# Six hand-overs between engines in a two-network float32 kernel

## The reference

```
for i in 0, 1:                                   # first network
    mix = latent attention + stick-breaking attention      (i = 0)
        = forgetting attention, 16 heads                   (i = 1)
    x = layer_norm(a * x + mix)
    x = layer_norm(a * x + (silu(x w1) * (x w3)) w2)       # width 2816
    x = x + sigmoid(x w_gate + b) * (p w_proj)
mod = silu(c) w_ada + b_ada                      # second network, conditioned by c
h   = modulate(rms_norm(x), mod)
mix = [retention(4 heads), sparse attention(8 heads)] w_out
      # sparse attention: compressed + selected + window branch, each gated
x   = x + ga1 * mix
h   = modulate(rms_norm(x), mod)
x   = x + ga2 * experts(h)    # 16384 single-row experts, 8 heads choose 16 each
return rms_norm(x)
```

## Time and profile before

| | us |
|---|---|
| median of 3 runs | 1767.23 |
| lowest and highest | 1764.0, 1768.93 |
| profiled execution, its own time | 1767.16 |
| its span | 1765.6 |
| PE busy | 1711.5 |
| DVE busy | 1314.8 |
| ACT busy | 968.7 |
| POOL busy | 230.2 |

### The profile page before, as it was taken

The page is one execution under the profiler, slowest core; times in us unless marked ns, Lnnn a source line. Parts: engine busy times, 40 slices in busy tenths (PEclk is TensorE's granted clock), DMA queues, the critical chain, the costliest instruction groups (busy, mean ns, idle before and its releaser), DMA issues.

```text
span 1765.6 us, 30099 instructions
## 1 busy us (share of the span) xinstructions
PE 1711.5 (97%) x10188; PEld 1508.3 (85%) x10188; DVE 1314.8 (74%) x2519; ACT 968.7 (55%) x1782; POOL 230.2 (13%) x158
## 2 busy tenths in 40 slices
PE   9899999999999998998989999999999999999998
PEld 8778888799888887897989999999998887888886
DVE  5468877777779777867667794888997666666666
ACT  5645554465555543556445546988885444333333
POOL 2010000013200000122115786000000000000001
PEclk9999999999999999999999999999999999999999
DMA  7524757655547676444234455444445555555554
GB/s 243 183 111 154 264 190 264 224 168 203 191 139 265 208 268 236 156 144 143 84 108 156 168 184 174 144 144 144 143 144 181 188 190 181 196 194 190 192 196 136
DMA packets 86354, 317.49 MB, mean 180 GB/s; under 512 B 9632, under 2 KB 9904, under 8 KB 85488
## 3 DMA queue, kind: packets, MB, share of 16 engines
q1 hardware_dynamic: 77328, 279.48, 47.0%
q10 hardware_dynamic: 7200, 25.45, 4.0%
q0 software_dynamic: 1728, 11.25, 1.8%
HBM read 315.08 MB, written 1.05 MB: 179 GB/s over the span
## 4 chain that ended last, share of the span: by engine, by line
PE 63%; DVE 7%; ACT 5%; issue 2%; DMA 1%; POOL 0%; ACTq 0%; DVEq 0%; POOLq 0%
PE bank L260 12%; PE bank L262 12%; PE bank L261 12%; PE bank L2163 9%; PE bank L2167 5%; PE bank L1147 5%; PE bank L2393 3%; DVE wl L199 2%; PE bank L1151 2%; ACT wh L192 2%; DMA ada<-in_w_ada 1%; PE bank L353 1%; DVE ss_s L595 1%; ACT ss_p L603 1%; ACT ss_p L601 0%
## 5 line engine op out<-in xcount | busy, mean ns | idle before, releaser
L192 ACT ACTIVATE wh<-ring 128x1024 fp32r<-128x1024 f32 x526 | 555.7, 1058 | 564.3 <-PE bank L262 362.2
L199 DVE TENSOR_TENSOR wl<-ring,wh 128x1024 fp32r<-128x1024 f32 x476 | 586.5, 1235 | 286.2 <-ACT wh L192 284.9
L260 PE MATMUL bank<-wh,xs 128*128 128x512 f32 (+1 forms) x796 | 286.3, 360 | 3.3 <-DVE wl L199 2.5
L262 PE MATMUL bank<-wh,xs 128*128 128x512 f32 (+1 forms) x796 | 282.1, 354 | 0.0
L261 PE MATMUL bank<-wl,xs 128*128 128x512 f32 (+1 forms) x796 | 282.1, 354 | 0.0
L2163 PE MATMUL bank<-xs,wh 128*128 128x512 f32 x736 | 250.8, 402 | 0.0
L1147 PE MATMUL bank<-xs,wh 128*128 128x512 f32 x704 | 223.0, 396 | 3.7 <-DVE xs L381 2.3
L260 PE MATMUL bank<-xs,wh 128*128 128x256 f32 x632 | 182.0, 288 | 1.8 <-DVE xs L381 0.9
L262 PE MATMUL bank<-xs,wl 128*128 128x256 f32 x632 | 178.8, 283 | 0.0
L261 PE MATMUL bank<-xs,wh 128*128 128x256 f32 x632 | 178.7, 283 | 0.0
L260 PEld LDWEIGHTS bank<-wh,xs 128*128 128x128 f32 x796 | 151.9, 191 | 27.5 <-DVE wl L199 5.0
(11 more groups left out here) (481 smaller groups left out, 2820.8 us busy)
## 6 DMA issues: line engine op xcount, KB each, us to landing
ring<-in_stream SPq DMA_DIRECT2D x529, 512.0 KB, 3.3
ada<-in_w_ada ACTq DMA_DIRECT2D x48, 512.0 KB, 4.7
rows<-in_rows POOLq DMA_DIRECT2D x1, 2560.0 KB, 11.4
rows<-in_rows POOLq DMA_DIRECT2D x2, 1024.0 KB, 5.0
con<-in_early POOLq DMA_DIRECT2D x1, 1374.0 KB, 14.4
x_feature_major<-in_x_fm SPq DMA_DIRECT2D x4, 256.0 KB, 6.7
x<-in_x_tm POOLq DMA_DIRECT2D x1, 1024.0 KB, 5.2
weighted<-in_subkeys POOLq DMA_DIRECT2D x1, 1024.0 KB, 5.3
```

The source lines that it names most:

```text
L192: C.activation(wh[q % AHEAD][:, :], ring[slot][:, :], ACT.Copy).then_inc(s_high, 1)
L199: low.tensor_tensor(wl[q % AHEAD][:, :], ring[slot][:, :], wh[q % AHEAD][:, :], ALU.subtract).then_inc(s_low, 1)
L260: T.matmul(o, left[0], right[0], start=start, stop=False, skip_group_check=True)
L262: return T.matmul(o, left[1], right[0], start=False, stop=stop, skip_group_check=True)
```

## The change

Six edits, none of which adds or removes arithmetic:

1. The barrier behind the logarithms of the first mixer waits for what was issued before them, and for ACT's logarithms no longer.
2. In both feed-forwards the two `residual_half` calls move from between the projections into the second one, behind its pieces 0 and 2.
3. The turning of the selected keys ks moves from between the two pieces of rq0 to between the two pieces of kw.
4. In step 1 of the last stream the rope of rq1 moves behind two compressed pieces and the low part of the window.
5. In step 4 `cmp_values` moves behind the last compressed piece of the keys and its row copy.
6. In `pair` the parts of the next up tile move ahead of the weighing of this down tile.

```diff
--- before.py
+++ after.py
@@ -291,13 +291,15 @@
     def no_need(k):
         pass
 
-    def project(left, nk, dst, width=HALF, need=no_need, hold=False, by_token=False):
+    def project(left, nk, dst, width=HALF, need=no_need, hold=False, by_token=False, behind=()):
 
 
         if width == HALF:
             for j in range(nk // 2):
                 done = two_k(dst, j, nk, left, need_x if left[0] is xh else need, hold and 2 * j + 2 == nk,
                              by_token and 2 * j + 2 == nk)
+                if j % 2 == 0 and j // 2 < len(behind):
+                    behind[j // 2]()
             return done
 
         def products(h, l):
@@ -896,10 +898,12 @@
         for t, b in ((0, 2), (1, 6)):
             sv_in = dve.did(V.tensor_copy(apart(sbv, slice(t, t + 1)),
                                           bank[b][:, :].rearrange("p (t h d) -> p t h d", t=1, h=NH)))
+        before_logs = issued()
         for h0 in range(0, NH, 2):
             act.wait(ex[h0 + 1])
             ln = act.did(C.activation(lz[:, h0:h0 + 2, :], lz[:, h0:h0 + 2, :], ACT.Ln, bias=1.0))
-        release()
+        for lane in (act, dve, pool):
+            lane.wait(*before_logs)
         scope.close()
 
         for lane in (pe, dve):
@@ -1256,9 +1260,8 @@
         gated_in = lambda k: pe.wait((s_gate, 5 * max(k + 1, KF - 2)))
         ada["of"] = (3, 4) if layer else (1, 2)
         y = project((hh, hl), KF, sums[0:2], need=gated_in)
-        for t in range(NT):
-            residual_half(z, st, 0, t, y, sums[t])
-        y = project((hh, hl), KF, sums[2:4], need=gated_in, hold=True, by_token=True)
+        behind = [lambda t=t, y=y: residual_half(z, st, 0, t, y, sums[t]) for t in range(NT)]
+        y = project((hh, hl), KF, sums[2:4], need=gated_in, hold=True, by_token=True, behind=behind)
         return first_token["done"], y, sums, (phh, pll, p_ready)
 
     GATES, PROJS = ([bank[3], bank[5]], [bank[6], bank[7]]), ([bank[0], bank[2]], [bank[1], bank[4]])
@@ -1680,7 +1683,9 @@
                                     .broadcast_to([P, 2, 2, DH]), ACT.Copy))
     vs_in = act.did(C.activation(nvs[:, :, :, DH:P], by_token(bank[3])[:, :, P:QC].rearrange("p t (g d) -> p t g d", g=2), ACT.Copy))
     turn_quarter("nq1", 1, bank[0], nqT[:, 2:4, :], read["nq1"])
-    y = both(bank[4])
+    quarter(bank[4], (xh, xl), 0, need_x)
+    turn_key_apart("ks", bank[0], added["ks"], turned_in["nq1"])
+    y = quarter(bank[4], (xh, xl), 4, need_x)
     pair_ab = rope_quarter("kw", bank[4], 2, DH, "n", y)
     doubled("kw", *pair_ab, 0)
     act.wait(read["kw"])
@@ -1694,7 +1699,6 @@
     turn_shifted("kc", bank[3], added["kc"], vs_in)
     pe.wait(ga1_done)
     quarter(bank[6], (xh, xl), 0, need_x, meantime=lambda y: windows_low("vc"))
-    turn_key_apart("ks", bank[0], added["ks"], turned_in["nq1"])
     y = quarter(bank[6], (xh, xl), 4, need_x)
     rotated_quarter("rq0", bank[6], 2, RDK, "r", y, 2)
     turn_key_apart("kw", bank[1], added["kw"], turned_in["nq0"])
@@ -1943,12 +1947,12 @@
             product["rq1"] = quarter(bank[7], (xh, xl), 4, need_x,
                                      meantime=lambda y: windows_sum("kc", "pe_k", added["win", "vc"]))
         elif st == 1:
-            rotated_quarter("rq1", bank[7], 2, RDK, "r", product["rq1"], 3)
             windows_high("kc")
             pe.wait(gd)
             cmp_piece("vc", 0, bank[5])
             cmp_piece("vc", 1, bank[5])
             windows_low("kc")
+            rotated_quarter("rq1", bank[7], 2, RDK, "r", product["rq1"], 3)
         elif st == 2:
             cmp_piece("vc", 2, bank[5])
             cmp_piece("vc", 3, bank[5])
@@ -1961,9 +1965,9 @@
             cmp_piece("kc", 1, bank[6])
         elif st == 4:
             cmp_piece("kc", 2, bank[6])
-            cmp_values(bank[5])
             cmp_piece("kc", 3, bank[6])
             cmp_row("kc", bank[6])
+            cmp_values(bank[5])
         elif st == 5:
             pe.wait(turned_in["rq1"])
             quarter(bank[7], (xh, xl), 0, need_x)
@@ -2547,10 +2551,9 @@
         q = q1 + 2 * u
         down_wide(q, s, u + LEAD, n)
         split(q + AHEAD, i)
-        weigh(q, s, u, n, first=i is None and u < 3)
-
         V.wait_ge(s_weighed, n + u)
         parts(u + 1, n, None if i is None and u < 2 else q - 2, s)
+        weigh(q, s, u, n, first=i is None and u < 3)
         if i is None and u == 0:
             T.wait_ge(s_wm, ROUTES)
         up(q + 1, s, u, n)
```

## The result

The changed kernel takes 1756.68 us (median of 6 runs, 1755.57 to 1761.0) against 1768.43 us for the kernel before in the same comparison (6 runs, 1764.0 to 1770.08). The ratio is 0.9949, 95% interval 0.9931 to 0.9966: some 9 us faster. The forecast was 1760.4 with a range of 1755 to 1766. The saving came out above the 6.8 us forecast in both comparisons, but 6.8 us lies within both intervals (6.0 to 12.2 us and 4.8 to 10.2).

A forecast was written before the change was run, and what follows sets the result against it. TensorE, busy 97% of the span, was taken as the bound. Terms 1.4 + 0.8 + 1.9 + 0 + 1.6 + 0.4 = 6.1 us plus 0.7 for the clock gave 1767.2 - 6.8 = 1760.4 us, range 1755.0 to 1766.0.

The forecast's parts named there:

- My term for the keys: Selected keys, last mixer: turning them sooner wins 1.9 us of a 2.40 us gap and 1.7 us lost clock; bounds 0.8 to 2.4.
- the 0.7 us: Whole kernel: net gain from falls of the clock beside the closed gaps, with one new long gap possibly bringing one.
- the 0.8 foretold: Behind the first mixer's barrier: TensorE's gap of 1.87 us falls to about 0.8 us.
- Rival (d): Barrier: the change does nothing there, as the softplus still waits for the logarithms; 1.4 us missing; 25% shared with another rival.
- The upper bound of 3.1: Barrier: most the edit could win, 3.1 us, with the fall of the clock gone; the term itself was 1.4 us.
- The slack of 0.6 us: Second feed-forward: the following low part, done at 671.1, comes 0.6 us before PE wants it, if the weights have landed.
- cost nothing there: Selected keys: four transposes and two copies move to where ACT and DVE wait for PE, at no cost.
- Both gaps as foretold: Rope, last stream: gaps of 2.05 and 2.27 us become about 1.4 and 2.8, same total, so 0 gain.
- by this rule alone: Rope: DVE operations with both inputs in SBUF and GpSimd SBUF reads exclude each other; new order would win 1.0 us; not taken.
- rival (a): Clock: falls go beyond the count, above all the one at 838 us; 3.4 us more, 1757.0 us; 15%.
- PE never waits: Expert loop: ACT waits 1.58 us for PE in each pair, PE never, so nothing is won inside the loop.
- Rival (c): Expert loop: weighing behind 0.7 us of parts delays each of 28 pairs, 19.6 us in all, 1780.0 us; 5%.

The follow-up runs named there:

- both comparisons: Unchanged changed kernel against the kernel before, timed twice: 1756.68 against 1768.43 us, ratio 0.9949; later 1759.90 against 1767.32 us, ratio 0.9957.
- the rope put back: Changed kernel with the rope of rq1 back at its old place: 1758.83 us, ratio to before 0.9954.
- the rope in the slot: Changed kernel with rq1's rope moved to where DVE waits for the third unit's exponentials, its transposes one step later: 1757.82 us, ratio to before 0.9956.
- the kernel before with the gap bridged: Kernel before with eight unused identity transposes added on TensorE in the 1.65 us gap before rk0's transposes: 1764.94 us, ratio 0.9991.
- all three mixer edits: Kernel before with only the keys, rope and values edits of the last mixer: 1762.52 against 1767.04 us, ratio 0.9989.
- the outer edits: Kernel before with only the barrier, residual sums and pair edits, none in the last mixer: 1762.08 us, ratio 0.9974.

## Why the prediction was right

The direction and the range were right, and so was, in the main, the mechanism of each edit but that on the keys. That the gaps summed up as forecast is partly luck: the keys came out 1.4 us too high, and feed-forward, rope and pairs together 1.1 to 1.9 us too low. My term for the keys also held the fall of the clock behind its gap, so the 0.7 us was not all that I had put down to the clock. Gap parts below are taken between profiles with equal low clock in the stretch; each rests on few profiles, and the edits of barrier, feed-forward and pairs were timed together only.

| place | forecast | gaps, measured | from |
|---|---|---|---|
| barrier | 1.4 | 1.4 | mean of five 109.80, of nine 108.37 |
| feed-forward | 0.8 | 1.3 to 1.9 | 17.72 to 18.32, now 16.40 |
| keys | 1.9 | 0.5 | 74.75 to 74.27 |
| rope | 0 | 0.2 to 0.4 | 34.59 to 34.15, see the rope put back |
| values | 1.6 | 1.7 | 34.88 to 34.38, 21.65 to 20.41 |
| pairs | 0.4 | 0.8 | 598.2 to 597.4 |
| sum | 6.1 | 5.9 to 6.7 | |
| clock, net | 0.7 | about 2 | below |

**Barrier.** Right as worked out, 0.77 us of gap for the 0.8 foretold. Rival (d) falls. The upper bound of 3.1 does not exist: the low clock behind the barrier costs nothing. In three of the five profiles with the old order it came already at 79 us, ahead of the 1.87 us gap, which was then gone. Three of the nine profiles with the change have 3.4 us of it there and take 108.37 to 108.40 us, the other six 108.34 to 108.37. TensorE's gaps over the stretch come to 8.5 us in these six and to 7.0 to 7.1 in the three: the slower matmuls take up time in which it would have waited.

**Feed-forward.** The term was too small for two reasons. I took the gap from one profile: in the five profiles with the old order it is 1.07, 1.42, 1.42, 1.65 and 1.83 us, as the conditioning weights land sooner or later; in the nine with the new order there is none, and the stretch is 16.40 us in each (the fifth of the old ones, 20.30 us, has a fall of the clock in it). And closing a gap wins some 0.25 us more than the gap's own length: 17.72 - 16.40 = 1.32 us for the gap of 1.07, 1.68 for that of 1.42 and 1.92 for that of 1.65, as the shown gap begins at the modelled end of a matmul, which in an unbroken run overlaps the next. The slack of 0.6 us that I worked out behind the second low part sufficed in all of them.

**Keys.** This step failed. I said that the four transposes "cost nothing there" at their new place, and that the clock's fall behind the gap goes. The transposes take 0.5 us of TensorE ahead of everything that ACT and DVE wait for there. The following low part and high part show it (before, with the next low part and the rope, then after):

```profile
775.76 1.23 DVE L199 TENSOR_TENSOR wl<-ring,wh 128x1024 fp32r<-128x1024 f32 x1 [2.61 <-ACT wh L192]
...
779.78 0.60 PE L1624 MATMUL bank<-keep,kdup_kw 128*128 128x128 f32 x4
779.82 1.06 ACT L192 ACTIVATE wh<-ring 128x1024 fp32r<-128x1024 f32 x1
...
780.91 1.23 DVE L199 TENSOR_TENSOR wl<-ring,wh 128x1024 fp32r<-128x1024 f32 x1 [1.51 <-ACT wh L192]
...
784.15 0.69 DVE L1571 TENSOR_TENSOR rope_n<-bank,con 128x512 f32<-128x512 f32 x1
```

```profile
771.83 1.22 DVE L199 TENSOR_TENSOR wl<-ring,wh 128x1024 fp32r<-128x1024 f32 x1 [2.61 <-ACT wh L192]
...
775.30 0.60 PE L1627 MATMUL bank<-keep,kdup_kw 128*128 128x128 f32 x4
...
775.88 2.01 ACT L192 ACTIVATE wh<-ring 128x1024 fp32r<-128x1024 f32 x2
...
776.97 2.36 DVE L199 TENSOR_TENSOR wl<-ring,wh 128x1024 fp32r<-128x1024 f32 x2 [1.51 <-ACT wh L192]
```

The two come 3.93 and 3.94 us earlier, when TensorE at the transposes of kw is 4.48 us earlier. Behind them DVE wins 0.96 us (from the low part at 780.91 to the rope 3.24 us before, from that at 776.97 to the rope at 779.25 2.28 after), and so the rope comes 4.90 us earlier, 0.4 more than TensorE's own shift, not 0.8. The new gap of 2.15 us was foretold to 0.05 us, and it is what keeps the edit at 0.5 us. The rest of my 1.9 was the fall of the clock, which can be there with either order: the first profile of before has it (75.80), the second has not (74.75), and the rope in the slot, which has the keys edit, has it again (75.66). So it costs 1.05 us with the old order and 1.4 with the new, and where it falls the edit wins 0.2 us at most, by this one profile.

**Rope.** Both gaps as foretold (1.4 and 2.8; 1.65 and 2.73), the whole 0.2 to 0.4 us better. The two low parts, apart from POOL's sum, take 2.36 us together and the sum 1.26, against 3.44 and 2.19 in the earlier trace rows, so the price of running together that the Trainium skill (SBUF — State Buffer, Who interferes with whom) leads one to expect is in the trace; by this rule alone the edit would have won 1.0. It won 0.2 to 0.4, as DVE then stood 0.56 us waiting for ACT's high part (791.75 above) before the low parts.

**Values.** The gap part was right, 1.7 for 1.6. Behind it stood more: where the clock falls after the 1.65 us gap, it costs 3.16 us (24.81 against 21.65). The fall stood in two of the four profiles with that gap and in none of the ten without it, one of which is the kernel before with the gap bridged. That suggests, and fourteen profiles can't show, that the gap makes the fall likelier without making it certain. Half of 3.16 is 1.6 us; the times agree with that (1.6 us won by bridging the gap, 2.2 us won by the values alone beyond their gaps), but their intervals also hold nothing for either. If it is so, my rival (a) was half right and should have entered the sum at half its price.

**Pairs.** I missed half. The step from "PE never waits" in the loop overlooked the loop's start: the first up product waited 0.17 us for its low part, and the parts ahead of the weighing win 0.4 us there (the gap and, as in the feed-forward, 0.25 us more) as they do at the end. Rival (c) falls: the 28 pairs lost nothing.

**Clock.** I priced each fall at 1.7 us for 3.4 us of low clock. It costs that only where TensorE is what everything waits for: 3.16 us for 6.8 at the compressed scores, about 1.8 for 3.4 in the one feed-forward that had it (20.30 us with a gap of 1.83), 1.05 to 1.4 for 3.4 in the first unit, 0.0 to 0.2 at 802 us in units 2 to 4 (34.88 with and without), nothing behind the barrier or at 880 to 890 us (the stretch from 850 to 900 us takes 49.5 us with 3.4 and 49.3 to 49.6 with 6.8). Over the runs, the low time worked out from each run's granted clock (twice one minus the clock, times the span) is 30 to 32 us in the mean before, and 25 and 27 us in the two sets of the changed kernel; the clock is given to 0.001, which is 3.5 us of low time in a single run. In the 33 runs of before that go with the first experiments the span rises by 0.36 us with each us of it (a straight line through them); 5 us less is 1.8 us, an estimate. With the gaps that makes 7.7 to 8.5 us, about what the two comparisons show. Which edit takes the low time away is not shown: it is 28.5 us with the values alone, where before had 32.2, but 30.3 with all three mixer edits, where before had 30.2, and 26.7 with the outer edits. What I drew from the Trainium skill (TensorE: Matmul & The Clock Gate, What's actually happening), whose statement is that the gate's bookkeeping does not start anew with the kernel, was that a fall at a given gap may be there in one execution and not in the next, and this agrees with these traces: 24.81 and 21.65 us for the same gap.

**What stays open.** The comparisons lie 0.8 and 2.2 us above the forecast saving, less than their intervals, so the times alone don't show that the clock was undersized. 1.5 us of the difference of the two profiles lies in stretches that the change doesn't touch. From 183.6 to 317.9 us one and the same instructions take 134.3 us in five profiles and up to 138.1 in the others, and around the layer norms at 336 and 698 us it is 49.3 to 51.3 and 34.3 to 38.0. Pieces of the stream and of the conditioning weights land there sooner or later, and whether the changed kernel does so less often can't be told from fourteen profiles.

## What to carry to other kernels

Price a hand-over by the whole ring it sits in: where ACT, DVE and TensorE wait for each other in turn, closing one gap of TensorE opens the next (2.40 became 2.15; when 2.15 went, 1.65 became 3.12), and what counts is by how much the slowest engine's chain gets shorter, less what the moved instructions cost at their new place. Compare stretches between the same two instructions at equal clock, not spans: with the new order those of the feed-forward and of the pairs repeat to 0.1 us (16.40 us nine times, 597.36 to 597.42) where the times scatter by 5. Where engines wait for each other in turn, add up neighbouring stretches, as one can gain what the next loses. And where a gap has a fall of the clock behind it in one profile, enter it with a probability, from more than one profile if they are to be had.

## What was new about the hardware

Time at the low clock can be free: 3.4 us of it in the softmax stream behind the barrier changed the stretch by 0.03 us in the mean, as TensorE's gaps there shrank from 8.5 to 7.1 us. And a closed gap of TensorE was worth 0.25 us more than the profile shows for it (1.32 us for 1.07, 0.42 for 0.17). Its place changes between executions of one program (84, 337, 699, 784, 838 and 890 us in one profile of the kernel before, 79, 704, 803 and 891 us in the other); only two places, near 700 and near 885 us, had it in twelve and in all of the fourteen profiles. A gap of 1.65 us that was partly filled with 1.04 us of otherwise useless transposes had no fall behind it, but neither had the unfilled gap in two of four profiles.
